# MLP weights of a two-block network: two ring slots filled by one transfer in place of two

## What is computed

```python
# D_MODEL = 2048, D_FF = 8192, x: (1, 256, 2048), all float32
h = rms_norm(x, g_mlp[l])
x = x + jnp.square(jax.nn.relu(h @ w_mlp_up[l])) @ w_mlp_down[l]
return rms_norm(x, g_final)
```

## Time and profile before

| | us |
|---|---|
| median of 3 runs (lowest to highest) | 2190.81 (2189.62 to 2191.64) |
| the profiled execution | 2190.26 |
| its span, first to last instruction | 2188.1 |
| TensorE matmul busy in it | 2169.3 (99%) |
| GpSimd busy | 1708.9 (78%) |
| VectorE busy | 1077.1 (49%) |
| ScalarE busy | 1036.9 (47%) |
| the MLP's transfers, first to last issue | 1458.1 to 2162.0 |

### The profile page before, as it was taken

The page is one execution under the profiler, slowest core; times in us unless marked ns, Lnnn a source line. Parts: engine busy times, 40 slices in busy tenths (PEclk is TensorE's granted clock), DMA queues, the critical chain, the costliest instruction groups (busy, mean ns, idle before and its releaser), DMA issues.

```text
span 2188.1 us, 34228 instructions
## 1 busy us (share of the span) xinstructions
PE 2169.3 (99%) x12539; PEld 1865.9 (85%) x12539; DVE 1077.1 (49%) x1835; ACT 1036.9 (47%) x1482; POOL 1708.9 (78%) x721
## 2 busy tenths in 40 slices
PE   8999999999999999999999999999999999999998
PEld 7888889888888888888888888888888888888887
DVE  5994243115753153758585645217605803822842
ACT  5434455454557545545454644454333333333343
POOL 7888868877667886657575658888888888888886
PEclk9999999999999999999999999999999999999999
DMA  7666555555454664545464546656566666666664
GB/s 236 191 188 189 182 154 173 185 167 176 139 155 164 222 179 137 151 122 164 126 166 133 154 142 187 210 183 188 188 195 189 191 192 192 188 193 192 187 192 154
DMA packets 321440, 383.86 MB, mean 175 GB/s; under 512 B 14654, under 2 KB 255781, under 8 KB 321061
## 3 DMA queue, kind: packets, MB, share of 16 engines
q1 hardware_dynamic: 317237, 377.80, 56.8%
q10 hardware_dynamic: 4080, 4.33, 0.6%
HBM read 379.98 MB, written 2.10 MB: 175 GB/s over the span
## 4 chain that ended last, share of the span: by engine, by line
PE 96%; DVE 1%; issue 1%; POOL 1%; DMA 1%; ACT 0%; ACTq 0%; POOLq 0%; DVEq 0%
PE lin_ps L2130 37%; PE lin_ps L2133 18%; PE lin_ps L2156 10%; PE lin_ps L2158 10%; PE lin_ps L2157 10%; POOL w_lo L621 1%; PE lin_ps L2329 1%; PE lin_ps L2327 1%; PE lin_ps L2328 1%; PE ps L2094 1%; PE ps L2633 1%; PE ps L2472 0%; PE ps L2644 0%; DVE ps L1826 0%; PE ps L2642 0%
## 5 line engine op out<-in xcount | busy, mean ns | idle before, releaser
L621 POOL TENSOR_TENSOR w_lo<-raw,w_hi 128x1024 fp32r<-128x1024 f32 x716 | 1708.6, 2395 | 463.4 <-ACT w_hi L655 354.7
L2130 PE MATMUL lin_ps<-a,w_hi 128*128 128x512 f32 x2176 | 697.0, 402 | 0.7 <-POOL w_lo L621 0.3
L655 ACT ACTIVATE w_hi<-raw 128x1024 fp32r<-128x1024 f32 (+1 forms) x456 | 475.2, 1053 | 462.1 <-PE lin_ps L2133 252.3
L2133 PEld LDWEIGHTS lin_ps<-a,w_lo 128*128 128x128 f32 x2176 | 408.7, 188 | 96.2
L2130 PE MATMUL lin_ps<-b,w_hi 128*128 128x512 f32 x1376 | 432.7, 396 | 0.8 <-DVE z L1478 0.8
L2133 PE MATMUL lin_ps<-a,w_lo 128*128 128x256 f32 x2176 | 428.2, 278 | 0.0
L666 ACT ACTIVATE w_hi<-raw 128x1024 fp32r<-128x1024 f32 x228 | 242.1, 1062 | 385.6 <-PE lin_ps L2133 226.4
L2130 PEld LDWEIGHTS lin_ps<-a,w_hi 128*128 128x128 f32 x2176 | 333.2, 189 | 7.3 <-issue 3.2
L2133 PEld LDWEIGHTS lin_ps<-b,w_lo 128*128 128x128 f32 x1376 | 258.5, 188 | 61.0
L2156 PE MATMUL lin_ps<-w_hi,a 128*128 128x512 f32 x752 | 293.4, 390 | 0.0
L2158 PE MATMUL lin_ps<-w_hi,a 128*128 128x512 f32 x752 | 292.7, 389 | 0.0
(11 more groups left out here) (428 smaller groups left out, 2150.4 us busy)
## 6 DMA issues: line engine op xcount, KB each, us to landing
raw<-in_w_in SPq DMA_DIRECT2D x144, 512.0 KB, 3.7
raw<-in_w_mlp_up SPq DMA_DIRECT2D x128, 512.0 KB, 3.7
raw<-in_w_mlp_down SPq DMA_DIRECT2D x128, 512.0 KB, 4.1
raw<-in_even_w_in SPq DMA_DIRECT2D x112, 512.0 KB, 3.7
raw<-in_odd_w_in SPq DMA_DIRECT2D x40, 512.0 KB, 3.7
raw<-in_even_w_out SPq DMA_DIRECT2D x32, 512.0 KB, 3.9
raw<-in_odd_w_out SPq DMA_DIRECT2D x32, 512.0 KB, 4.6
raw<-in_w_o SPq DMA_DIRECT2D x32, 512.0 KB, 4.1
```

Of the source, the lines that this page charges most:

```text
L621: nc.gpsimd.tensor_tensor(w_lo[:, slot, 0:width], raw[:, slot, 0:width], w_hi[:, slot, 0:width].bitcast(F32), ALU.subtract).then_inc(lo_do ...
L655: nc.scalar.activation(w_hi[:, slot, 0:width], raw[:, slot, 0:width], ACT.Copy).then_inc(hi_done, 1)
L2130: nc.tensor.matmul(lin_ps[:, 2 * parity + m, :], hi[:, k, m * P:(m + 1) * P], src[:, kk].rearrange("p s n -> p (s n)"), start=(q == 0 and ...
L2133: last = nc.tensor.matmul(lin_ps[:, 2 * parity + m, 0:T], lo[:, k, m * P:(m + 1) * P], src[:, kk, 0, :], start=False, stop=(q == n - 1 and ...
```

## The change

The 128 units of `w_mlp_up` and the 128 of `w_mlp_down` are loaded in 128 pairs. One transfer of 1 MB fills two neighbouring slots (0 and 1, or 2 and 3) of `raw`. All other stages, and what ScalarE, GpSimd and TensorE compute with a unit, stay as they are.

```diff
+            def load_pair(u, slot, src):
+
+                sp.wait_ge(lo_done, u - SLOTS + 2)
+                sp.dma_start(raw[:, slot:slot + 2].rearrange("p s n -> p (s n)").rearrange("p (k n) -> p k n", k=src.shape[1]),
+                             src).then_inc(raw_in[slot], 16)
+
-            def stream(name, u0, groups, kus, col0=0, row0=0, per=2):
+            def stream(name, u0, groups, kus, col0=0, row0=0, per=2, paired=False):
...
+                        if paired:
+                            for q in range(0, kus, 2):
+                                j = g * kus + q
+                                k0 = row0 + q * UK
+                                load_pair(base + j, (u0 + j) % SLOTS, v[:, k0:k0 + 2 * UK, bass.ds(col + (col0 + g * UN), UN)])
+                            continue
...
-            def stream_out(name, u0, row0=0):
+            def stream_out(name, u0, row0=0, paired=False):
...
+                if paired:
+                    for n in range(NB):
+                        for j in range(0, 8, 2):
+                            k0 = row0 + 2 * j
+                            load_pair(u0 + 8 * n + j, (u0 + j) % SLOTS, v[:, k0:k0 + 4, _block(n)])
+                    return
...
-                stream("w_mlp_up_2", UNIT0["mlp"] + 64 * ph, 8, 4, col0=ph * D)
-                stream_out("w_mlp_down_2", UNIT0["mlp"] + 64 * ph + 32, row0=ph * DC)
+                stream("w_mlp_up_2", UNIT0["mlp"] + 64 * ph, 8, 4, col0=ph * D, paired=True)
+                stream_out("w_mlp_down_2", UNIT0["mlp"] + 64 * ph + 32, row0=ph * DC, paired=True)
...
-                act.wait_ge(raw_in[slot], 16 * (u // SLOTS + 1))
+                act.wait_ge(raw_in[slot - slot % 2 if u >= UNIT0["mlp"] else slot], 16 * (u // SLOTS + 1))
...
-                        act.wait_ge(raw_in[slot], i * 16 + 16 * ((u0 + s) // SLOTS + 1))
+                        act.wait_ge(raw_in[slot - slot % 2 if u0 >= UNIT0["mlp"] else slot], i * 16 + 16 * ((u0 + s) // SLOTS + 1))
```

## The result

| | us |
|---|---|
| the changed kernel, median of 4 runs (lowest to highest) | 2228.32 (2227.18 to 2229.36) |
| the kernel before beside it, median of 4 | 2191.0 (2189.62 to 2191.64) |
| ratio, 95% interval | 1.0170 (1.0158 to 1.0182) |
| predicted | 2219 (2197 to 2248) |

The change costs 37.3 us, 1.7%. The profiled execution has a span of 2227.4 us, 39.3 more than before. About 2 of these lie ahead of the MLP: the last issue for the stage in front of it stands at 1457.38 us, and at 1455.32 before. Two executions differ that much in the opening, whatever the kernel, so the MLP's share of the profiled execution is 37.2.

The account below looks back on a forecast made before the run. TensorE was taken as the bound, its matmuls busy for 2169.3 of 2188.1 us. Up rounds losing 5.8 us and down rounds 23.0, with end effects, gave 2190.3 + 28.9 = 2219 us, range 2197 to 2248.

Parts of the forecast that it names:

- The bound and the room: MLP: TensorE sets the end; a slot's loop takes 7.75 us (down) or 7.5 (up) against rounds of 10.88 and 11.15.
- The loop of a pair: Two slots in the MLP: `w_hi` start to `w_lo`, two `w_lo`, issue, transfer; 6.05 + L us down, 6.18 + L up.
- signs that I had named for being wrong: MLP profile: L under 4.9 us, `w_lo` longer than 2.40 us when in pairs, or waits sitting elsewhere.
- L: Time from issue to landing of a pair's 1 MB transfer in the MLP: 5.15 us up, 5.55 down.
- The threshold: MLP: the pair's loop keeps up with TensorE only if L is at most 4.83 us (down) or 4.97 (up).
- The sum: MLP: 32 up rounds lose 0.18 us each, 32 down rounds 0.72 each; together 28.8 us.
- the worse transfer: Rival, MLP loads: L is 5.9 us up and 6.3 down, 78 us lost, 2268; counted 2236 to 2275, chance 0.16.
- halfway: Milder case of the worse transfer in the MLP: L 5.5 us up, 5.9 down; 53 us lost, 2243.
- The cushion: Between `w_lo` and its turn on TensorE: 4.5 us of lateness not felt at once; 0.3 us free in the last column.
- No change: Rival, MLP: the loop keeps up, L at or under 4.83, TensorE never waits; 2188 to 2196 us, chance 0.12.
- The better transfer: Rival, MLP loads: the second half costs 1.35 us or less, start and completion paid once; 2196 to 2206 us, chance 0.12.
- The clock: Rival, MLP: a waiting TensorE could be granted 1.2 in place of 2.4 GHz; clock or longer still, chance 0.02.

Follow-up runs that it names:

- e8: The changed kernel with eight slots of `raw` in the MLP, four more in the free part of `z`, transfers still 1 MB; 2193.56 us, ratio 1.0011.
- e9: The changed kernel with each pair's transfer bringing only 768 KB, the last quarter left out; 2191.14 us, ratio 1.0001.
- e3: The changed kernel with two 512 KB transfers behind the pair's one late wait, each unit waiting for its own; 2191.01 us, ratio 1.0001.
- e4: The changed kernel with each pair's 1 MB as two 512 KB transfers on one semaphore, both units waiting for both; 2230.20 us, ratio 1.0182.
- e5: The changed kernel with two 512 KB transfers, each issued as early as before the change, both units waiting for both; 2191.15 us, ratio 1.0000.
- e1: The changed kernel with only the up units paired, the down units loaded singly as before; 2203.36 us, ratio 1.0057.
- e2: The changed kernel with only the down units paired, the up units loaded singly; 2194.85 us, ratio 1.0018.

## Why the prediction was right, and where its sizes were off

**The bound and the room.** Right. TensorE set the end, the load path had room, and the change spent it. e8 shows the other side: with more slots the same transfers cost nothing in the steady state, and nothing is gained either, as TensorE was never waiting.

**The loop of a pair.** Right in form. Its parts stand in the round shown above. Two small parts were left out: 0.12 us from the landing to `w_hi`, and single `w_lo` in the up phases that take up to 2.86 us (the median stays 2.41; the last section shows beside what). The second is one of the signs that I had named for being wrong, and it came in part. With the first alone the up loop is 6.25 + L in the round shown (11.95 - 5.7).

**The threshold.** Right as far as it was measured: 4.83 and 4.97 us were worked out (0.12 less each with the part left out), e9 loses nothing at 4.4 and 4.6, and no run lies closer from below.

**L, the term that was mis-sized.** The step was "the landing of today plus that", that is plus 1.45 us. In up it gave 5.15, and 5.6 was measured; in down it gave 5.55, and 5.1 was measured. The 1.45 us themselves are real: in e3 the second of two queued transfers lands 5.3 - 3.9 = 1.4 us after the first. Two things don't hold. One larger transfer doesn't end where two queued ones would: in up it is later and in down earlier (5.6 and 5.1, against 5.4 and 5.5 in the pairs of e4). And the landing of today in down was no firm base. The 4.1 us are the median of one execution. In e5, where single loads of 512 KB are issued at the same places, it is 3.6:

```profile
raw<-in_w_mlp_down SPq DMA_DIRECT2D x128, 512.0 KB, 3.6
```

So a further 512 KB cost 1.9 us in up (5.6 - 3.7), and in down 1.0 or 1.5, by which of the two executions is taken as the base. Why the landing in down differs between them is open.

**The sum.** Up rounds were predicted to lose 0.18 us each and lose 0.72 (11.87 - 11.15) in the phase shown; down rounds were predicted to lose 0.72 and lose 0.52 (11.40 - 10.88). Times 32 each, that is 23.0 + 16.6 = 39.7 us, near the 37.2 of the MLP. I had named down as the expensive half. It is up. That the predicted 28.8 came within 8 us is in part luck: the two errors of L, 0.45 us too little in up and 0.45 too much in down, cancel over 32 rounds each. Most of the 8 us is what was put at nothing, by an estimate from the round shown: 0.12 us from landing to `w_hi` in each of 64 rounds is 7.7 us, and the longer `w_lo` come on top.

Three of the rivals' sums hold slips. For the worse transfer the down rounds lose 6.05 + 6.3 - 10.88 = 1.47 us and not 1.52, halfway 1.07 and not 1.12, so 77 and 51 us in place of 78 and 53. For the better one with down at 5.15 the sum is 10.2 + 2.6 = 13 us and not 16. The forecast doesn't rest on them, and no bound moves by more than 3 us.

**The cushion.** It was right that it exists, about how large it is (4.5 us read, 4.3 by e1), and that the last column's two passes leave nothing of it: e2 loses 3.7 us, nearly all in the last column. TensorE's stalls begin earlier than forecast, not in the first down phase but at the end of the first up phase, since eight up rounds at 0.72 us are 5.8 us and use it up alone. This is the first wait for `w_lo` in the MLP:

```profile
1550.24 0.73 PE L2148 MATMUL lin_ps<-b,w_hi 128*128 128x512 f32 x2 [0.53 <-POOL w_lo L639]
```

For the sum it hardly counts, as the cushion is used up once.

**The rivals.** No change is out: the shortest landing in the phases shown is 4.9 us. The better transfer is out by the time; its landing came in down (5.1 us, where it had 5.15 to 5.45) and not in up. The worse transfer was half right, in up. The fit of the Trainium skill ("DMA: Bandwidth & Descriptors", "Anatomy of one DMA — SWDGE path") gave an estimate of 1.20 us for the further 512 KB. For these transfers, issued on another kind of queue, the traces have 1.0 to 1.5 in down and 1.9 in up, so one figure for both doesn't do. The Trainium skill advises at least 1 MiB per DMA for bandwidth (same page, "Rules for kernel authors"). That bought nothing here: the DMA engines were busy for 0.60 of the MLP before, and e4 shows that the same bytes in two transfers of 512 KB cost as much time. The clock that was granted stayed at 1.00, the 2.4 GHz level, in spite of the waits:

```profile
1460.00:2219.00 759.00, 738.27 (x3668) 613.35 (x3667) 193.90 (x188) 269.43 (x289) 624.52 (x260) 1.00 0.56 178
```

## What to carry to other kernels

In a ring of buffers, count the loop of one buffer: issue, landing, every step that reads it, and back to the issue; merging two loads makes the loop longer by the second step and by the second load's bytes, and it costs nothing until it is longer than the time in which the consumer goes once round the ring, and then it costs the difference in every round. If loads are merged to save issues, give each part its own completion (e3) or the ring more slots (e8). A saving on a queue that nobody waits for is worth nothing, and two such edits are not to be added up one by one, since they share one cushion.

## What the hardware showed that I had not expected

VectorE's operations on the squares in the up phases run much faster when GpSimd pauses. One cast of 128 x 512 in the kernel before, beside a `w_lo`, and one in the changed kernel, in the hole between two pairs of `w_lo` (1869.64 lies between the end of a pair at 1868.94 and the next start at 1870.73); then the groups of all 32 casts of both kernels (busy, mean ns), and of the operation that reads its input from `lin_ps`:

```profile
1501.90 2.39 DVE L2044 CAST a<-scr 128x512 f32 x1 [0.16 <-DVE scr L2042]
...
1869.64 0.43 DVE L2062 CAST a<-scr 128x512 f32 x1 [0.16 <-DVE scr L2060]
...
1870.73 4.79 POOL L639 TENSOR_TENSOR w_lo<-raw,w_hi 128x1024 fp32r<-128x1024 f32 x2 [1.79 <-ACT w_hi L684]
...
L2044 DVE CAST a<-scr 128x512 f32 x32 | 77.9, 2434 | 5.1 <-DVE scr L2042 5.1
...
L2062 DVE CAST a<-scr 128x512 f32 x32 | 34.0, 1064 | 5.1 <-DVE scr L2060 5.1
...
L2058 DVE TENSOR_REDUCE scr<-lin_ps 128x512 f32<-128x1024 f32 x32 | 39.2, 1224 | 204.6 <-PE lin_ps L2151 204.6
```

2.39 us against 0.43, for the same operation on the same shape. The mean over all 32 casts fell from 2.43 to 1.06 us: in the changed kernel 22 take 0.43 us, 19 of them wholly in a hole, and the 10 that run almost wholly beside a `w_lo` take 2.38 to 2.60. Before, all 32 do so and take 2.38 to 2.45. The operation that reads `lin_ps` takes 1.22 us, as it did before. VectorE has time here, so it earned nothing, but in a kernel that is bound by VectorE the same holes in GpSimd's work could. That has not been tried.

It goes the other way too, and `w_lo` is in the loop of a pair: these are its longer ones, 22 in the up phases and 4 right behind them. All 26 `w_lo` of the changed kernel's MLP that take over 2.5 us start while VectorE is at one of these operations. One of them, with the operation that still runs for 0.6 us beside its start:

```profile
1670.02 2.31 DVE L2060 SCALAR_TENSOR_TENSOR scr<-scr 128x512 f32<-128x512 f32 x1
...
1671.74 2.85 POOL L639 TENSOR_TENSOR w_lo<-raw,w_hi 128x1024 fp32r<-128x1024 f32 x1
```

Before, no `w_lo` of the MLP takes more than 2.51 us. No run takes VectorE's work away, so what this costs in a round is not measured.
